# A gated MLP fed with x times the norm's weights, its factor applied to the products, and weight splits kept two tiles ahead beside modulation rows

## Chip, cores and metric

The kernel runs on one core of one Trainium2 chip. The metric is the device time of one execution in microseconds (us): the median of several runs. TensorE is called PE (its weight loads PEld), VectorE DVE, ScalarE ACT, GpSimd POOL, SyncE SP.

## What is computed

A first block of two layers, and then a second block of two layers, on 256 tokens of width 1024 in fp32 (the first block carries 256 context tokens too). Cut to what matters here:

```python
def first_block(...):
    for l in range(DEPTH):                                 # DEPTH = 2
        mod_x = silu(c) @ w_ada[l] + b_ada[l]              # 6 * 1024 modulation values, for x
        mod_c = silu(c_ctx) @ w_ada[l] + b_ada[l]          # and for the context
        ...attention, x = x + gt1 * (o @ w_out[l])
        hx2 = rms_norm(x, g_norm2[l]) * (1 + sc2) + sh2
        x = x + gt2 * conv_ffn(hx2, ...)

def second_block(...):
    for l in range(DEPTH):
        ...four branches, merged
        x = x + rms_norm_2(merged @ w_out[l], norm_mix_post[l])
        h2 = rms_norm_2(x, norm_ffn_pre[l])                # x * rsqrt(mean(x*x) + eps) * g
        f_g, f_u = split(h2 @ w_ffn_in[l], 2)              # 2 * 2816 columns
        f = (silu(f_g) * f_u) @ w_ffn_out[l]
        x = x + rms_norm_2(f, norm_ffn_post[l])
```

The factor `rsqrt(mean(x*x))` is one number for each token, so `h2 @ w` equals `((x * g) @ w)` times that number.

## The kernel before

Activations lie transposed: 8 chunks of 128 channels by 256 tokens. A product in fp32 accuracy is three matmuls in fp32r: weights and activations are each the sum of a rounded high part and a low part, and hi*hi, hi*lo and lo*hi are added (`products`, L396 to L398). One weight tile is 128 x 1024 (8 blocks of 128 x 128) and gives 128 output channels with 24 matmuls.

**The stream of weights.** All weights come as one list of 704 tiles of up to 512 KB. SP loads tile i into one of NRAW = 6 raw buffers as soon as the tile six before it is used up (for a tile that is to be split: when its low part is made; for a modulation tile, which is never split: when its matmuls are done). The tiles to be split then go through ACT (high part, L968) and DVE (low part, L1572) into one of NSPLIT = 4 buffers, which come free when the matmuls of the tile four before are done. Every engine runs through the same program order with its own `Feed`. `Feed.next()` is called where a tile is used, and there it issues, in order, the splits that are due: up to five list places ahead of the tile in use, as long as the buffer's last user has been released.

```python
    def next(self):
        i = self.n
        self.n += 1
        while self.cut < min(i + NRAW, self.total) and self.room():
            if self.cut in self.place:
                self.split(self.cut)
            self.cut += 1
        return i
```

The queues of ACT and DVE are thus in this order by hand: a split stands where `next` was called, with its wait on the load (ACT) or on the high part (DVE), and what comes after it waits behind it.

**Modulation rows.** `ada_step` takes two weight tiles, does 8 fp32 matmuls with 2 active rows (L482), and DVE copies the 128 x 256 result out of PSUM (L1634). One call later `ada_turn` has PE transpose it in two halves (L467), and DVE adds four pieces of 32 rows (L1619) and the bias (L1622). 8 steps are at the start; the others are put between the units of the first block's attention, one for each unit, until they are used up: 12 beside layer 0's first stream, 12 beside its second, 10 beside layer 1's (4 and 2 more stand just ahead). During attention they are the only tiles of the stream; the output projection's 8 tiles follow in the list. In one attention unit PE does the scores (L572), the turn of the row before (L467), values (L606, L611), transposes of probabilities (L591) and then the matmuls of the next modulation row (L482). DVE's queue in the same unit: maxima, the copies out of PSUM (L1771 among them), then the splits of `next`, then the copy of the row (L1634).

**Output projection** of the first block: for each of 8 tiles DVE adds to the residual x (L1582, XT<-ps), ACT squares it (L1006), and PE sums the squares (L453). ACT's queue begins with the load of the Sqrt table (`warm`, L996), and then has for each tile: `next` (splits), square. DVE's has: `next` (splits), residual. After the eighth tile come the root (ACT L1024), its reciprocal (DVE L1608), and the norm.

**The gated MLP of the second block**, layer l: `post_add` on DVE updates x in four pairs of chunks (L2224, L2229). ACT squares each chunk (L1006), PE sums the 8 squares with a matrix of ones in fp32 (L453), ACT takes the root (L1024), DVE the reciprocal (L1608), DVE multiplies x by weight and factor (`norm2`, L1582), ACT makes the high parts (L1326), DVE and POOL the low ones (L1999, L2284). PE's first two tiles (`two_tiles`) do the parts that need high parts alone (L410, L411), 32 matmuls, and then those with low parts (L416), 16. From then on 22 steps j have a gate tile, an up tile and a tile of the down projection five steps behind. Between them: ACT Silu of the gate product (L1553), DVE times the up product (L2243), POOL the high and the low part (L2539, L2541).

## Time and profile before

| | |
|---|---|
| median of 3 runs | 2309.62 us (2307.52 to 2311.8) |
| profiled execution, its own time | 2310.19 us |
| its span, first to last instruction | 2308.1 us |
| mean granted clock of TensorE | 0.965 |
| PE busy | 2141.5 us (93%) |
| DVE busy | 1552.1 us (67%) |
| ACT busy | 1151.8 us (50%) |
| POOL busy | 489.6 us (21%) |
| DMA | 378.21 MB, mean 164 GB/s |

Engines overlap, so the shares don't add up. Where PE is busy without a break, only fewer or shorter matmuls help; elsewhere the time is set by the chain that ends each of its waits. The clock is that of the matmul array, as a share of 2.4 GHz; at 0.50 a matmul takes twice the time between starts.

### The profile page before, as it was taken

The page shows a single profiled execution, that of the slowest core. Times are in us where ns is not written, and L with a number is a line of the kernel's source. Part 1 is how long each engine was busy: PE and PEld are TensorE (multiplying, and loading weights), DVE is VectorE, ACT ScalarE, POOL GpSimd, SP SyncE. Part 2 cuts the span into 40 slices and gives each one's busy share as a digit, 9 for nine tenths or more (in the row PEclk, how much of TensorE's full clock was granted, in tenths as well). Part 3 has the DMA queues.
Part 4 walks back from the last instruction along what each step waited for, and adds up shares of the span by engine and source line. Part 5 has one row for each costly group of instructions (what it writes and reads, how often), then busy time and mean ns, then how long its engine had stood idle before and what let it go on. Part 6 is the DMA issues. An engine that isn't in the chain of part 4 may idle for free.

```text
span 2308.1 us, 42283 instructions
## 1 busy us (share of the span) xinstructions
PE 2141.5 (93%) x17432; PEld 1970.9 (85%) x17432; DVE 1552.1 (67%) x2301; ACT 1151.8 (50%) x1917; POOL 489.6 (21%) x628
## 2 busy tenths in 40 slices
PE   6999979999999998899998989989998999998998
PEld 3985549999999995589997889989997888998997
DVE  3657766777777756667776769756555677965554
ACT  3534444555655642555556555554444655554443
POOL 0011330333233002213321043202110124311110
PEclk8999999999999998999999999999999999998999
DMA  8535444555465443335553435544553433553552
GB/s 325 164 128 220 165 183 146 178 195 177 155 201 185 153 165 128 147 119 188 187 190 104 157 104 191 173 138 164 185 190 103 146 128 129 165 185 127 191 191 84
DMA packets 103199, 378.21 MB, mean 164 GB/s; under 512 B 11584, under 2 KB 11744, under 8 KB 101984
## 3 DMA queue, kind: packets, MB, share of 16 engines
q1 hardware_dynamic: 101520, 367.31, 46.7%
q10 hardware_dynamic: 1488, 8.20, 0.9%
q8 instruction: 139, 2.28, 0.4%
q14 instruction: 52, 0.43, 0.1%
HBM read 374.42 MB, written 1.05 MB: 163 GB/s over the span
## 4 chain that ended last, share of the span: by engine, by line
PE 35%; issue 8%; DVE 6%; POOL 3%; ACT 3%; POOLq 0%; DVEq 0%; ACTq 0%
PE ps L396 10%; PE ps L397 10%; PE ps L398 10%; DVE WL L1572 2%; PE ps L453 2%; POOL R L2521 1%; POOL R L2479 1%; ACT WH L968 1%; DVE RST L1608 1%; DVE TMP L1582 1%; PE ps L410 1%; DVE R L1582 1%; PE ps L411 1%; PE ps L416 0%; POOL X L2284 0%
## 5 line engine op out<-in xcount | busy, mean ns | idle before, releaser
L396 PE MATMUL ps<-X,WH 128*128 128x256 f32 x4384 | 1243.4, 284 | 13.6 <-DVE WL L1572 12.5
L397 PE MATMUL ps<-X,WH 128*128 128x256 f32 x4384 | 1228.7, 280 | 0.0
L398 PE MATMUL ps<-X,WL 128*128 128x256 f32 x4384 | 1225.8, 280 | 0.0
L1572 DVE TENSOR_TENSOR WL<-RAW,WH 128x1024 fp32r<-128x1024 f32 (+2 forms) x608 | 802.7, 1340 | 461.3 <-ACT WH L968 460.6
L396 PEld LDWEIGHTS ps<-X,WH 128*128 128x128 f32 x4384 | 826.9, 189 | 28.3 <-DVE WL L1572 17.6
L397 PEld LDWEIGHTS ps<-X,WH 128*128 128x128 f32 x4384 | 827.4, 189 | 1.4
L398 PEld LDWEIGHTS ps<-X,WL 128*128 128x128 f32 x4384 | 827.1, 189 | 0.0
L968 ACT ACTIVATE WH<-RAW 128x1024 fp32r<-128x1024 f32 (+2 forms) x608 | 625.7, 1047 | 383.7 <-PE ps L398 362.5
L1106 ACT ACTIVATE PB<-ps,SM 128x512 f32<-128x512 f32 (+1 forms) x152 | 87.7, 584 | 156.4 <-DVE SM L1745 156.2
L2326 POOL TENSOR_SCALAR R<-CONS,SM 128x128 f32<-128x128 f32 x128 | 84.4, 670 | 360.5 <-DVE SM L1755 360.5
L2418 POOL TENSOR_TENSOR TMP<-TMP 128x256 f32<-128x256 f32 x66 | 49.0, 742 | 438.3 <-ACT TMP L1288 434.8
L1582 DVE SCALAR_TENSOR_TENSOR TMP<-ps,PARS,TMP 128x255 f32<-128x255 f32 x264 | 124.2, 480 | 9.5 <-ACT TMP L1284 0.6
L1582 DVE SCALAR_TENSOR_TENSOR R<-R,PARS 128x256 f32<-128x256 f32 x180 | 109.5, 660 | 0.0
L2423 POOL TENSOR_TENSOR X<-TMP,X 128x256 fp32r<-128x256 f32 x66 | 104.0, 1576 | 5.3
L1284 ACT ACTIVATE TMP<-ps,PARS 128x256 f32<-128x256 f32 x132 | 71.4, 555 | 55.9 <-PE ps L398 52.8
L410 PE MATMUL ps<-X,WH 128*128 128x256 f32 x208 | 64.4, 337 | 25.5 <-ACT X L1326 14.0
L1745 DVE TENSOR_REDUCE SM<-ps 128x1 f32<-128x512 f32 (+2 forms) x136 | 77.1, 605 | 14.5 <-PE ps L572 13.9
L1288 ACT ACTIVATE TMP<-TMP 128x256 f32<-128x256 f32 x66 | 27.8, 421 | 113.1 <-DVE TMP L1582 113.1
L606 PE MATMUL ps<-PTB,R 128*64 128x128 f32 x768 | 61.5, 293 | 24.4 <-ACT PTB L1121 16.8
L606 PEld LDWEIGHTS ps<-PTB,R 128*64 128x64 f32 x768 | 44.8, 143 | 45.5 <-issue 20.5
L482 PE MATMUL ps<-RAW,R 128*32 128x256 f32 x768 | 62.3, 444 | 22.3 <-DVE R L1619 8.5
L2539 POOL CAST X<-TMP 128x256 fp32r<-128x256 f32 x44 | 19.4, 442 | 282.1 <-DVE TMP L2243 282.1
(184 smaller groups left out, 2157.5 us busy)
## 6 DMA issues: line engine op xcount, KB each, us to landing
RAW<-w_dram SPq DMA_DIRECT2D x674, 512.0 KB, 3.8
RAW<-w_dram SPq DMA_DIRECT2D x16, 480.0 KB, 3.1
BIG<-big_dram ACTq DMA_DIRECT2D x4, 1024.0 KB, 5.1
RAW<-w_dram SPq DMA_DIRECT2D x8, 320.0 KB, 2.7
RAW<-w_dram SPq DMA_DIRECT2D x6, 384.0 KB, 3.0
XT<-x_dram ACTq DMA_DIRECT2D x2, 1024.0 KB, 10.9
CONS<-con_dram ACTq DMA_DIRECT2D x1, 1105.0 KB, 5.0
out_dram<-XT SPq DMA_DIRECT2D x1, 1024.0 KB, 3.9
```

Source lines behind the costliest of these rows:

```text
L396: e.matmul(out, a.hi, b.hi, start=start and i == 0, stop=False, skip_group_check=open_bank)
L397: e.matmul(out, a.hi, b.lo, start=False, stop=False, skip_group_check=open_bank)
L398: last = e.matmul(out, a.lo, b.hi, start=False, stop=stop and i == n - 1, skip_group_check=open_bank)
L410: e.matmul(b.ap[:, 0:256], w.hi[:, c], src[c].hi, start=c == 0, stop=False)
L606: e.matmul(ob[0].ap[64 * s:64 * s + 64, c:c + 128], u["subs"][s]["v"][j], b[:, 128 * j:128 * j + 128], start=j == 0, stop=j == nk - 1)
L968: e.activation(weights(i).hi, raw(i), ACT.Copy).then_inc(*w_hi.mark(i))
L1106: e.activation(ap, bank.ap[:, x * u["nk"]:x * u["nk"] + u["nk"]], ACT.Exp, bias=sm.ap[:, col:col + 1], accum_out=sm.ap[:, 4 + col:5 + col] ...
L1572: e.tensor_tensor(weights(i).lo, raw(i), weights(i).hi.bitcast(F32), ALU.subtract).then_inc(*w_lo.mark(i))
L1582: return e.scalar_tensor_tensor(out=out, in0=a, scalar=s, in1=b, op0=o0, op1=o1)
L1745: e.tensor_reduce(sm.ap[:, col:col + w], bank.ap[:, 0:w * nk].rearrange("p (x n) -> p x n", x=w), AX, ALU.max, negate=True).then_inc(*maxe ...
L2326: e.tensor_scalar(d.ap, ident, sm.ap[:, 8 + s:9 + s], None, ALU.mult).then_inc(*inverted.mark(tag, i, s))
L2423: e.tensor_tensor(a.ap.lo, bg.ap, a.ap.hi.bitcast(F32), ALU.subtract).then_inc(*gate_lo.mark(tag, j))
```

## The change

1. In the second block the MLP's input is x times the norm's weights: ACT makes the high parts straight from x with the weight as scale, in pairs, as `post_add` finishes them, then the squares of the same pair; DVE makes the low parts. PE starts the first two tiles' high parts at once, then sums the squares (`between`), then does the low parts. The factor goes on the gate product twice: DVE multiplies it out of PSUM (`scaled`), ACT takes the Silu in place, POOL multiplies the result by the factor again (`pooled`), which stands for the factor of the up product; DVE times the up product as before. So per step j there is one DVE and one POOL instruction more, and Silu waits for DVE; the 8 multiplications of `norm2` and its 8 copies become 8 scaled copies.
2. Beside modulation rows after the first eight, `Feed.next` splits up to two places ahead (`ahead=3`) and not five.
3. The turn of a modulation row is two fp32 matmuls with a 128 x 2 picking matrix as moving operand, which sum the four pieces as well; DVE's reduction is gone, the bias is added straight from PSUM.

```diff
@@ class Feed
-    def next(self):
+    def next(self, ahead=NRAW):
         i = self.n
         self.n += 1
-        while self.cut < min(i + NRAW, self.total) and self.room():
+        while self.cut < min(i + ahead, self.total) and self.room():
...
@@ tensor: two_tiles(src, at, between=None)
                         e.matmul(b.ap[:, 0:256], w.lo[:, c], src[c].hi, start=False, stop=False)
+                if between is not None:
+                    between()
                 for b, i in zip(bk, us):
...
@@ tensor: ada_turn, ada_step
                 for h in range(2):
-                    last = e.transpose(bank.ap[:, 256 + 128 * h:384 + 128 * h], b.ap[:, 128 * h:128 * h + 128], ident)
+                    last = e.matmul(bank.ap[:, 256 + 2 * h:258 + 2 * h], b.ap[:, 128 * h:128 * h + 128], con("pick"), start=True, stop=True)
                 last.then_inc(*adaturn.mark(l, c))
-                bank.free = [modded("sum", l, c)]
+                bank.free = [modded(l, c)]
-            def ada_step(ring=PS):
+            def ada_step(ring=PS, ahead=3):
...
-                    i = feed.next()
+                    i = feed.next(ahead)
...
             for c in range(8):
-                ada_step()
+                ada_step(PS, NRAW)
...
@@ tensor: second block
-                ss = SquareSum(("fpre", l), 8)
-                for n in range(4):
+                ss = SquareSum(("fpre", l), 8, k.sq2[0])
+                for _ in range(8):
                     ss.add()
-                    ss.add()
-                    ss.flush(keep=2)
-                ss.rstd(k.rst[0])
-                feed_forward(("glu", l), parts2_of(("fpre", l)), lambda tag, j, half: (convd if half else gated)(tag, j, half))
+                feed_forward(("glu", l), parts_of(("fpre", l)), lambda tag, j, half: convd(tag, j, half) if half else scaled(tag, j),
+                             between=lambda: ss.rstd(k.rst[1]))
...
@@ scalar: second block
-                ss = SquareSum(("fpre", l), 8)
-                post_add(("post", l), ss)
-                ss.rstd(1024, k.rst[0])
-                norm2(("fpre", l))
-
-                def silu_gate(j, bk):
-                    (bank, i), _ = bk
+                k.rst[0].free = [scaled(("post", l), "s", 3)]
+                ss = SquareSum(("fpre", l), 8, k.sq2[0])
+                for n in range(4):
+                    q.wait_ge(*resid(("post", l), n))
+                    for c in (2 * n, 2 * n + 1):
+                        e.activation(H.hi[:, c], X2[:, c], ACT.Copy, scale=par("fpre", l)[:, c:c + 1]).then_inc(*x_hi.mark(("fpre", l), c))
+                    for c in (2 * n, 2 * n + 1):
+                        ss.add(X2[:, c])
+                ss.rstd(1024, k.rst[1])
+
+                def silu(j):
                     b = tmp.take()
-                    q.wait_ge(*lin(i))
-                    wait(b.free)
-                    e.activation(b.ap, bank.ap[:, 0:256], ACT.Silu).then_inc(*gated.mark(("glu", l), j, 0))
+                    q.wait_ge(*scaled(("glu", l), j))
+                    e.activation(b.ap, b.ap, ACT.Silu).then_inc(*gated.mark(("glu", l), j, 0))
                     b.free = [gate_lo(("glu", l), j)]
...
@@ vector: ada_turn
-                t = ADA[c % 2]
-                parts = bank.ap[:, 256:512].rearrange("p (h j m) -> p h m j", h=2, j=4)[:, :, 0:2, :]
-                e.tensor_reduce(t, parts, AX, ALU.add).then_inc(*modded.mark("sum", l, c))
-                q.wait_ge(*modded("sum", l, c))
+                parts = bank.ap[:, 256:260].rearrange("p (h s) -> p s h", h=2)
                 b_ada = par("b_ada", l)[:, 2 * c:2 * c + 2].unsqueeze(1).to_broadcast([128, 2, 2])
-                e.tensor_tensor(MODS[l][:, :, 2 * c:2 * c + 2], t.rearrange("p h s -> p s h"), b_ada, ALU.add).then_inc(*modded.mark(l, c))
+                e.tensor_tensor(MODS[l][:, :, 2 * c:2 * c + 2], parts, b_ada, ALU.add).then_inc(*modded.mark(l, c))
...
@@ vector: second block
-                ss.rstd(k.rst[0])
-                norm2(("fpre", l), par("fpre", l), recips(("fpre", l)))
+                for c in range(8):
+                    q.wait_ge(*x_hi(("fpre", l), c))
+                    stt(H.lo[:, c], X2[:, c], par("fpre", l)[:, c:c + 1], H.hi[:, c].bitcast(F32), ALU.mult,
+                        ALU.subtract).then_inc(*x_lo.mark(("fpre", l), c))
+                ss.rstd(k.rst[1])
+                bufs = {}
+
+                def silu_in(j, bk):
+                    b = bufs[j] = tmp.take()
+                    (bank, i), = bk
+                    q.wait_ge(*recips(("fpre", l)))
+                    q.wait_ge(*lin(i))
+                    wait(b.free)
+                    e.tensor_tensor(b.ap, bank.ap[:, 0:256], k.rst[1].ap, ALU.mult).then_inc(*scaled.mark(("glu", l), j))
 
                 def silu_gate(j, bk):
-                    b, (bank, i) = tmp.take(), bk[1]
-                    q.wait_ge(*gated(("glu", l), j, 0))
+                    b, (bank, i) = bufs.pop(j), bk[1]
+                    q.wait_ge(*pooled(("glu", l), j))
                     q.wait_ge(*lin(i))
...
-                feed_forward(("glu", l), silu_gate)
+                feed_forward(("glu", l), silu_gate, first=silu_in)
...
@@ gpsimd: second block
-                norm2(("fpre", l))
+                bufs = {}
+
+                def scale_gate(j):
+                    b = bufs[j] = tmp.take()
+                    q.wait_ge(*recips(("fpre", l)))
+                    q.wait_ge(*gated(("glu", l), j, 0))
+                    e.tensor_tensor(b.ap, b.ap, k.rst[1].ap, ALU.mult).then_inc(*pooled.mark(("glu", l), j))
...
@@ constants
+    put("pick", np.tile(np.eye(32)[:, 0:2], (4, 1)))
```

`feed_forward` on ACT, DVE and POOL gets an argument `first`, called when the gate tile's product is taken and before the `next` of the up tile.

## Rows read from the trace of the kernel before

**Rows 1.** Waits: engine, line, waited for: us in total, times, longest.

```profile
ACT WH L968 <- DMA RAW<-w_dram: 19.8, 8, 5.4
...
PEld ps L467 <- DVE R L1634: 55.4, 39, 6.7
```

**Rows 2.** Timeline of PE, layer 0, second stream: start, us, line, [idle before <- releaser].

```profile
290.29 1.07 PE L482 MATMUL ps<-RAW,R 128*32 128x256 f32 x16
...
293.69 1.07 PE L482 MATMUL ps<-RAW,R 128*32 128x256 f32 x16
...
295.32 0.44 PE L467 MATMUL ps<-CONS,R 128*128 128x128 f32 x2
...
305.56 1.07 PE L482 MATMUL ps<-RAW,R 128*32 128x256 f32 x16
...
312.30 0.69 PE L467 MATMUL ps<-CONS,R 128*128 128x128 f32 x2 [5.04 <-DVE R L1634]
...
329.83 0.70 PE L572 MATMUL ps<-R 64*128 64x256 f32 x4
```

**Rows 3.** Timeline of ACT in the same stretch.

```profile
309.60 1.06 ACT L968 ACTIVATE WH<-RAW 128x1024 fp32r<-128x1024 f32 x1 [5.10 <-DMA RAW<-w_dram]
```

**Rows 4.** Timeline of DVE in the same stretch.

```profile
293.80 0.69 DVE L1771 COPY PTB<-ps 128x512 f32<-128x512 f32 x1 [0.58 <-PE ps L591]
...
310.69 1.23 DVE L1572 TENSOR_TENSOR WL<-RAW,WH 128x1024 fp32r<-128x1024 f32 x1 [3.89 <-ACT WH L968]
```

**Rows 5.** Timeline of PE, layer 1's attention.

```profile
927.25 1.07 PE L482 MATMUL ps<-RAW,R 128*32 128x256 f32 x16
...
931.95 1.07 PE L482 MATMUL ps<-RAW,R 128*32 128x256 f32 x16
...
937.19 1.07 PE L482 MATMUL ps<-RAW,R 128*32 128x256 f32 x16
...
957.41 0.70 PE L711 MATMUL ps<-RST,CONS 32*128 32x256 f32 x4
...
965.00 1.13 PE L572 MATMUL ps<-R 64*128 64x512 f32 x4
```

**Rows 6.** Timeline of DVE, layer 1's output projection.

```profile
991.92 0.49 DVE L1582 SCALAR_TENSOR_TENSOR XT<-ps,SM,XT 128x256 f32<-128x256 f32 x1 [2.05 <-PE ps L398]
...
994.98 0.48 DVE L1582 SCALAR_TENSOR_TENSOR XT<-ps,SM,XT 128x256 f32<-128x256 f32 x1
...
1013.70 0.48 DVE L1582 SCALAR_TENSOR_TENSOR XT<-ps,SM,XT 128x256 f32<-128x256 f32 x1
```

**Rows 7.** Timeline of ACT, layer 1's output projection: end of the table's warming.

```profile
991.63 0.21 ACT L996 ACTIVATE SM<-CONS 128x1 f32<-128x1 f32 x1
```

**Rows 8.** Timeline of PE's weight loads, layer 0's second output projection.

```profile
389.30 0.19 PEld L396 LDWEIGHTS ps<-X,WH 128*128 128x128 f32 x1 [1.21 <-DVE WL L1572]
```

**Rows 9.** Timeline of all engines, start of the second block's first MLP.

```profile
1549.53 6.25 PE L453 MATMUL ps<-PB,CONS 128*128 128x256 f32 x16 [4.73 <-ACT PB L1006]
...
1558.63 2.01 ACT L1326 ACTIVATE X<-TMP 128x256 fp32r<-128x256 f32 x5 [2.34 <-DVE TMP L1582]
...
1559.19 0.55 PE L410 MATMUL ps<-X,WH 128*128 128x256 f32 x1 [3.42 <-ACT X L1326]
...
1565.76 2.04 PE L416 MATMUL ps<-X,WH 128*128 128x256 f32 x16
...
1567.65 0.28 PE L396 MATMUL ps<-X,WH 128*128 128x256 f32 x1
```

**Rows 10.** Busy time by windows: length, PE, PEld, DVE, ACT, POOL, PEclk, DMA share, GB/s.

```profile
1564.00:1566.00 2.00, 2.00 (x16) 2.00 (x14) 1.55 (x3) 0.56 (x1) 0.00 (x0) 0.77 0.00 0
...
1570.00:1740.00 170.00, 170.00 (x1446) 170.00 (x1445) 93.35 (x82) 69.39 (x81) 25.60 (x43) 1.00 0.56 189
```

**Rows 11.** One line of the kernel each: duration ns min/median/max, first and last start.

```profile
L2418 POOL TENSOR_TENSOR TMP<-TMP x66: 727/743/753, 403.9 to 1193.9; 128x256 f32<-128x256 f32 x66
```

**Rows 12.** The same view for the reduction of a modulation row.

```profile
L1619 DVE TENSOR_REDUCE R<-ps x48: 142/159/175, 14.4 to 963.5; 128x4 f32<-128x16 f32 x48
```

More of the change, by code:

```diff
@@ L987, in tile, with used @@
                 return PS.take(), i
-            def used():
-                i = feed.next()
+            def used(ahead=NRAW):
+                i = feed.next(ahead)
                 feed.release(i)
@@ L1135, in attend, with feed_forward @@
                 highs(units[n - 1]["tile"])
-            def feed_forward(tag, gate, early=None, late=None):
+            def feed_forward(tag, gate, early=None, late=None, first=None):
                 bk, steps = [], iter(())
@@ L1142, in feed_forward @@
                         bk.append(got.pop(0) if got else tile())
+                        if len(bk) == 1 and first is not None:
+                            first(j)
                         if len(bk) == 2:
@@ L1799, in attend, with feed_forward @@
                         invert(i)
-            def feed_forward(tag, gate, early=None, late=None):
+            def feed_forward(tag, gate, early=None, late=None, first=None):
                 bk, steps = [], iter(())
@@ L1806, in feed_forward @@
                         bk.append(got.pop(0) if got else tile())
+                        if len(bk) == 1 and first is not None:
+                            first(j, bk)
                         if len(bk) == 2:
@@ L2344, in feed_forward @@
                         bk += 1
+                        if bk == 1 and first is not None:
+                            first(j)
                         if bk == 2:
```

42 lines of the change are left out of this document (21 added, 21 removed).

## The prediction

> **What bounds the kernel now.** The first view is the page's busy time. PE is busy for 93% of the span, so the time is PE's work plus its waits. The next question is where PE is busy without a break, because there only its own work counts. The windows over a gated MLP answer it. PE has 170.00 us of work in 170 us, with DVE at 93.35, ACT at 69.39 and POOL at 25.60 [rows 10]. Instructions added on those three engines are free there as long as no wait reaches PE.
>
> Then the waits, for the gaps. Two belong to this change. ACT waited up to 5.4 us for a raw weight tile, and PE's loads for the transposed modulation row waited 55.4 us for DVE's copy of it [rows 1]. The timelines tie them together. Beside the last three modulation rows of layer 0's second stream, ACT's next entry is the split of an output projection tile that is not loaded yet. It idles 5.10 us and starts at 309.60 [rows 3]. DVE's low part follows at 310.69 after 3.89 us of idling [rows 4]. The copy of the modulation row stands behind that split, so PE stops for 5.04 us before L467 at 312.30 [rows 2]. The wait of an early split is thus paid by PE through two queues. The same happens beside layer 1's last rows.
>
> The third place is the start of the second block's MLP. PE idles 4.73 us before the sums of squares. It does them in 6.25 us, idles 3.42 us, and starts the first tile at 1559.19; its third tile starts at 1567.65 [rows 9]. It is also slow there: the granted clock is a mean of 0.77 in 1564 to 1566, against 1.00 in the loop behind [rows 10]. The 32 matmuls from 1559.19 to 1565.76 take 0.205 us each, and the 16 after them 0.118 [rows 9]. That is the 1.2 GHz level and the 2.4 GHz level.
>
> **Part 1: splits two ahead beside modulation rows.** Splits of the projection's tiles 1 to 4 were spread over the last three rows. Now only tiles 1 and 2 are split, both beside the last row, when their loads have had two units to land. Tiles 3 and 4 move to the start of the projection.
>
> *Layer 0, second stream.* An undisturbed unit takes 3.40 us (L482 at 290.29, again at 293.69). From L482 at 305.56 to the first scores after the last row, 329.83, are three units: 24.27 us in place of 10.20 [rows 2]. Surplus 14.07. What stays is a wait in the last unit. Let that unit begin at L482 = 0. ACT makes two high parts of 1.06, so the second is done at 2.1. DVE's copy L1771 ends at 0.8 (294.49 against 293.69), so its second low part runs from 2.1 to 3.35 (1.23 long). The copy of the row adds 0.38, which is the distance from the low part's end at 311.92 to L467 at 312.30: 3.75. L467 normally starts at 1.63. PE waits about 2.1 [rows 2 to 4]. Gain 14.07 - 2.1 = 12.0.
>
> *Layer 1.* A unit takes 4.70 us (927.25 to 931.95). From 937.19 to 965.00 are three units and one extra group of 0.63 (0.70 less the overlap): 27.81 in place of 14.73, surplus 13.08 [rows 5]. ACT has a copy of probabilities before the splits here, so I take 2.5 for the wait that stays. Gain 10.6. Both gains could be up to 2 smaller if splits and exponentials collide, and up to 2 larger if the remaining wait vanishes.
>
> *What it costs later.* In the projection, DVE's first residual now stands behind the low parts of tiles 3 and 4, and ACT's high parts for them start only after the table is warm, at 991.84 [rows 7]. Two high parts end at 993.95, the second low part at 995.2. So the first residual is at about 995.3 instead of 991.92, 3.4 late. Behind it, residual, square, high part and low part form a ring of one tile: 3.06 us (991.92 to 994.98). Before, the eighth residual came 21.78 us after the first (1013.70) [rows 6]; the ring alone needs 7 x 3.06 = 21.4. So 0.4 is caught up, and the eighth residual is 3.0 late. Root, reciprocal and norm hang on it with PE idle, so layer 1 pays 3.0. I add 0.5, because a longer pause leaves the array at 1.2 GHz for longer: 3.5. In layer 0 a second projection follows as cover. But PE already waits there for low parts (1.21 before one tile [rows 8]), so the delay passes through: 2.9. PE's tile 3 needs its low part 5.6 us after the projection starts, which is about when it is ready; a wait there costs 0 to 1.5 for each layer. If no delay were passed on, both costs would be 0.
>
> **Part 2: the start of the MLP, twice.** The first pair of chunks is ready as before, so PE begins at about 1549.5, but with tile 1 instead of sums. ACT makes 8 copies and 8 squares of 0.40 (five in 2.01 [rows 9]), somewhat less for squares: the last pair's copies end near 1554.5. PE's first tile trickles along with them and ends near 1555. Tile 2 is 16 matmuls of 0.205: 1558.3. The sums take 6.25 at 1.2 GHz and about half at 2.4. After the last pause the full clock came back some 5.7 us after work began, so it should come back during tile 2 or the sums here: I take 4.0 and get 1562.3. The low parts take 1.9: third tile at 1564.2 instead of 1567.65, a gain of 3.4. I count 3.0, since the first tile's gaps may delay the clock. Bounds: 1.2 with all sums at the low level, 5.7 with the full clock from 1555 on. Two layers: 6.0 (2.4 to 11.4).
>
> Root, reciprocal and the first multiplication now lie beside PE's low parts and third and fourth tiles; the fourth tile's split stands behind ACT's root and DVE's reciprocal, but is due two tiles later. In the loop DVE gets 22 more multiplications and POOL 22 more of 0.743 [rows 11] for each layer. DVE has 76 us free of 170 and POOL 144 [rows 10]: price nothing. If the cover were gone, 44 x 0.743 = 33 us would be due.
>
> The Trainium skill, page "SBUF — State Buffer" (the shared port pair), says that a GpSimd instruction and a DVE instruction with two SBUF inputs exclude each other, so the added POOL work could hold up DVE's splits. By that rule DVE loses at most the same 33 us over both loops, against 2 x 76 us free, so it would change nothing here.
>
> **Part 3: the modulation turn.** A pair of transposes takes 0.44 us [rows 2]. The new turn is two fp32 matmuls, each two instructions in this trace (the 8 modulation matmuls are x16). Lower bound: 1.07/16 = 0.067 each, 0.27 for four. Upper bound: as long as a transpose each, 0.88; two moving columns can't take longer than 128. Over 28 rows where PE is the bound that is -5 to +12. Each of the four still loads 128 columns, so I take no change. DVE loses a reduction of 0.16 [rows 12] in 34 rows. Most of it falls into idle time; I take 0.9 in all. PE's next row waits for the bank until the bias is added instead of the sum, which is the same place in DVE's queue.
>
> The Trainium skill, page "TensorE: Matmul & The Clock Gate", section "LDWEIGHTS (loading the stationary operand)", gives a load as columns / 1.2 ns: 107 ns for 128, whatever follows it. By it four loads make 0.43 us as an estimate, which speaks against any gain from the short moving operand. No row shows this shape; the sum above does not use it.
>
> **Sum.** -12.0 - 10.6 + 2.9 + 3.5 - 6.0 - 0.9 = -23.1 us. On the profiled execution's 2310.2 that is 2287.1; it lies 0.6 above the median, so 2286.5 for the median.
>
> **Rivals.**
> *The waits come back in the projections* (0.15). PE reaches tile 3 before its late split in both layers, and layer 0's second projection stays behind DVE: 4 to 5 us more in each layer. Speaking for it: the ring of 3.06 has almost no slack and PE already waits for low parts [rows 6, 8]. Against: PE's squares slow it to more than the ring. Time 2286.5 + 9 = 2295.5.
> *More is gained* (0.13): the array stays at 2.4 GHz around the sums, and the delay of the projection is absorbed. -23.1 - 5 - 4: 2277.5.
> *The distance does nothing* (0.05): ACT waits for the same loads later, so only parts 2 and 3 count, and the later splits' delay does not appear. -6.9: 2302.7.
> *Slower* (0.05): in the MLP loop Silu waits for DVE, POOL for Silu, DVE for POOL, and DVE's next split stands behind that. If the round trip exceeds its cover, every j is longer. It decides at 23.1/44 = 0.53 us for each j; if the 0.743 of POOL's new multiplication showed in full, the time is 2286.5 + 33 = 2319.5. Against it: DVE and ACT have 3.5 and 4.6 us free in each j [rows 10], and splits are three tiles ahead.
> *The forecast* (0.62): 2281 to 2292.
>
> The forecast, more gained and most of the first rival give the range 2277 to 2298. 0.2%, or 4.6 us, is about what a measurement of this kernel can tell from no change. Slower is the fourth rival, 0.05. Within it: 0.02, the part of the third rival in which part 2 gives its lower bound too. Faster: the rest, 0.93.
>
> **What the new profile would show.** ACT's splits with waits for RAW beside the last modulation rows gone, PE's waits before the turn at most 2.5 us. First residual of the projections about 3.4 us later behind the attention's end. At the MLP's start L410 before L453 and no 3.42 us gap. The MLP loops still with PE at 100%. Wrong would be: waits of PE for low parts in the projections above 2 us, a loop longer than before, or a turn that takes longer than 0.44.

## The result, and the profile after

The changed kernel takes 2294.34 us (median of 4 runs, 2292.43 to 2298.63) against 2308.57 for the kernel before on the same chip: ratio 0.994, 95% interval 0.9921 to 0.9959. That is 14.2 us less, where 23.1 were forecast (2286.5 us, range 2277 to 2298). The profiled execution of after took 2298.63, its span is 2296.8, so it is the slowest of its runs. One execution of experiment 10 (4141 us) and one of the kernel before beside it (4162 us) were disturbed, and no ratio counts them. In what follows, a difference between kernels is the ratio of the runs less one, times 2310 us, with its interval; a difference between places of two traces is said to be one.

The waits of the page after (engine, line, waited for: total, times, longest), beside [rows 1]:

```profile
PEld ps L468 <- DVE R L1636: 37.2, 39, 4.6
...
PE ps L395 <- DVE WL L1577: 21.9, 19, 2.8
...
PE ps L468 <- DVE R L1636: 13.2, 9, 4.1
```

L1636 is the copy of the row, L468 the new turn, L1577 the low part, L395 the first product. Beside the modulation rows ACT's waits for a raw tile are gone; 5.1 us of such waits are left, all in the first 40 us. The wait before the turn shrank and did not vanish. PE's wait for low parts over the whole kernel stood like this before:

```profile
PE ps L396 <- DVE WL L1572: 18.3, 16, 3.3
```

It grew by 3.6 us. Its long cases lie outside the first block's output projections, where none is longer than 1.2 us. PE's timeline in layer 0's second stream, beside [rows 2]:

```profile
311.45 1.07 PE L483 MATMUL ps<-RAW,R 128*32 128x256 f32 x16
312.45 0.70 PE L573 MATMUL ps<-R 64*128 64x256 f32 x4
313.09 0.61 PE L468 MATMUL ps<-CONS,R 128*128 128x2 f32 x4
313.62 0.66 PE L607 MATMUL ps<-PTB,R 128*64 128x128 f32 x8
...
315.01 1.07 PE L483 MATMUL ps<-RAW,R 128*32 128x256 f32 x16
...
318.58 1.07 PE L483 MATMUL ps<-RAW,R 128*32 128x256 f32 x16
...
323.53 1.01 PE L468 MATMUL ps<-CONS,R 128*128 128x2 f32 x4 [3.25 <-DVE R L1636]
324.47 1.12 PE L607 MATMUL ps<-PTB,R 128*64 128x128 f32 x8
...
326.99 1.23 PE L573 MATMUL ps<-R 64*128 64x256 f32 x4
```

Read the starts, not the durations, for the price of a stretch. From the turn's start to the next instruction are 0.53 us here (313.09 to 313.62; the median of the turns at the full clock is 0.54), and 0.37 before (L467 at 295.32, the next line at 295.69). The unit is 3.56 long (311.45 to 315.01), not 3.40. Behind the 3.25 us wait everything takes nearly twice as long: L607 1.12 for 0.66, L468 itself 1.01 for 0.61. The granted clock is 0.50 from the turn to the next scores. DVE and ACT in the last unit, beside [rows 3, 4]:

```profile
318.22 2.00 ACT L967 ACTIVATE WH<-RAW 128x1024 fp32r<-128x1024 f32 x2
```

```profile
318.98 1.29 DVE L1911 TENSOR_TENSOR X<-R,X 128x256 fp32r<-128x256 f32 x2
320.19 0.68 DVE L1773 COPY PTB<-ps 128x512 f32<-128x512 f32 x1
320.79 2.35 DVE L1577 TENSOR_TENSOR WL<-RAW,WH 128x1024 fp32r<-128x1024 f32 x2
323.06 0.41 DVE L1636 COPY R<-ps 128x256 f32<-128x256 f32 x1
```

ACT's two splits start without a wait for the load. But DVE had two low parts of the attention's output to make (L1911, 1.29 us) before its copy L1773, which ends at 320.9, 2.3 after the unit's start, where the prediction had put it at 0.8. The two low parts then follow in one piece, and the row's copy behind them.

Layer 1's projection on DVE, beside [rows 6]. From the scores behind the last row to the first residual are 30.95 us (962.11 to 993.06), against 26.92 before (965.00 to 991.92), so 4.0 more. Of these, 0.9 are the scores themselves, which run at the half clock here (962.11 to 964.02). In experiment 1 below, where they don't, it is 3.2 more. The ring is the same, 3.06:

```profile
990.78 2.36 DVE L1577 TENSOR_TENSOR WL<-RAW,WH 128x1024 fp32r<-128x1024 f32 x2 [2.96 <-ACT WH L967]
993.06 0.48 DVE L1587 SCALAR_TENSOR_TENSOR XT<-ps,SM,XT 128x256 f32<-128x256 f32 x1
...
996.12 0.48 DVE L1587 SCALAR_TENSOR_TENSOR XT<-ps,SM,XT 128x256 f32<-128x256 f32 x1
...
1014.46 0.48 DVE L1587 SCALAR_TENSOR_TENSOR XT<-ps,SM,XT 128x256 f32<-128x256 f32 x1
```

The start of the second block's first MLP, and the windows of its loop, beside [rows 9, 10] (length, then busy time of PE, PEld, DVE, ACT, POOL, then PEclk, DMA share, GB/s):

```profile
1551.85 0.55 PE L409 MATMUL ps<-X,WH 128*128 128x256 f32 x1 [4.91 <-ACT X L1549]
...
1555.99 0.58 PE L409 MATMUL ps<-X,WH 128*128 128x256 f32 x1 [0.19 <-ACT X L1549]
...
1560.42 4.00 PE L454 MATMUL ps<-R,CONS 128*128 128x256 f32 x16
1564.07 2.22 PE L417 MATMUL ps<-X,WH 128*128 128x256 f32 x16
1566.13 0.28 PE L395 MATMUL ps<-X,WH 128*128 128x256 f32 x1
```

```profile
1570.00:1740.00 170.00, 170.00 (x1460) 170.00 (x1459) 92.58 (x105) 71.47 (x84) 64.57 (x65) 1.00 0.56 193
```

The first tile starts where the sums stood, in steps of ACT's pairs, the sums take 3.7 us at a mean granted clock of 0.89, and the third tile starts 14.28 us after PE's wait (1551.85 to 1566.13), against 18.12 before (1549.53 to 1567.65). The loop is still all PE, with POOL at 65 in place of 26.

### The profile page after: what moved, and what is told of

Same layout as the page of the kernel before. It is cut to its first block, busy times and chain, and to the rows that moved or that the text cites. A ratio compares the mean times of both kernels' runs of the same rounds, so it can differ in the third digit from the quotient of the medians.

```text
span 2296.8 us, 42538 instructions
## 1 busy us (share of the span) xinstructions
PE 2151.5 (94%) x17528; PEld 1987.3 (87%) x17528; DVE 1532.2 (67%) x2285; ACT 1152.5 (50%) x1917; POOL 565.1 (25%) x668
## 4 chain that ended last, share of the span: by engine, by line
PE 36%; issue 8%; DVE 5%; POOL 3%; ACT 3%; POOLq 0%; DVEq 0%; ACTq 0%
PE ps L395 11%; PE ps L397 10%; PE ps L396 10%; DVE WL L1577 2%; POOL R L2539 1%; PE ps L454 1%; POOL R L2497 1%; ACT WH L967 1%; DVE RST L1613 1%; PE ps L409 1%; DVE R L1587 1%; PE ps L410 1%; PE ps L417 1%; DVE TMP L1587 1%; POOL X L2300 0%
## 5 line engine op out<-in xcount | busy, mean ns | idle before, releaser
L395 PE MATMUL ps<-X,WH 128*128 128x256 f32 x4384 | 1241.8, 283 | 16.9 <-DVE WL L1577 16.0
L1577 DVE TENSOR_TENSOR WL<-RAW,WH 128x1024 fp32r<-128x1024 f32 (+2 forms) x608 | 782.5, 1307 | 455.3 <-ACT WH L967 454.6
L395 PEld LDWEIGHTS ps<-X,WH 128*128 128x128 f32 x4384 | 826.2, 188 | 31.5 <-DVE WL L1577 21.2
L409 PE MATMUL ps<-X,WH 128*128 128x256 f32 x208 | 66.5, 344 | 29.2 <-ACT X L1549 10.6
L607 PE MATMUL ps<-PTB,R 128*64 128x128 f32 x768 | 60.8, 291 | 25.2 <-ACT PTB L1120 17.7
L2557 POOL TENSOR_TENSOR TMP<-TMP,RST 128x256 f32<-128x256 f32 x44 | 32.8, 745 | 209.6 <-ACT TMP L1557 209.6
L607 PEld LDWEIGHTS ps<-PTB,R 128*64 128x64 f32 x768 | 44.4, 142 | 41.5 <-issue 15.7
```

What stands on the lines that cost most here:

```text
L395: e.matmul(out, a.hi, b.hi, start=start and i == 0, stop=False, skip_group_check=open_bank)
L409: e.matmul(b.ap[:, 0:256], w.hi[:, c], src[c].hi, start=c == 0, stop=False)
L607: e.matmul(ob[0].ap[64 * s:64 * s + 64, c:c + 128], u["subs"][s]["v"][j], b[:, 128 * j:128 * j + 128], start=j == 0, stop=j == nk - 1)
L1577: e.tensor_tensor(weights(i).lo, raw(i), weights(i).hi.bitcast(F32), ALU.subtract).then_inc(*w_lo.mark(i))
```

## The experiments

ACT computes the same 32 square roots in every kernel, so their starts are milestones by which traces can be laid over each other. The table gives the start in the trace of before, and for each kernel the shift against it in us. Column heads are the experiments' numbers below. Experiment 10 isn't among them: its trace is that of the execution of 4141 us.

| root at | after | 1 | 2 | 3 | 4 | 5 | 6 | 7 | 8 | 9 | 11 | 12 |
|---|---|---|---|---|---|---|---|---|---|---|---|---|
| 157.4 | +0.7 | -0.9 | -1.3 | +2.6 | -0.5 | -0.7 | +6.8 | +0.5 | -0.1 | -0.7 | -1.4 | -0.5 |
| 226.0 | +3.8 | -1.0 | -2.2 | +9.2 | -0.6 | -0.8 | +18.1 | -0.2 | -0.2 | -0.1 | -2.3 | -0.5 |
| 298.3 | +5.8 | -2.4 | -2.3 | +8.9 | -2.0 | +0.6 | +21.5 | -0.6 | -0.2 | -1.5 | -3.7 | -0.7 |
| 370.2 | +0.6 | -8.1 | -2.6 | +11.5 | -7.8 | -4.0 | +17.2 | -6.9 | -9.8 | -8.0 | -9.5 | -7.6 |
| 829.3 | +1.9 | -8.4 | -2.8 | +11.5 | -8.2 | -2.8 | +17.1 | -6.9 | -10.1 | -8.1 | -9.9 | -7.7 |
| 1015.4 | +1.3 | -16.5 | +0.2 | +18.0 | -16.2 | -6.0 | +18.8 | -15.3 | -22.0 | -13.8 | -17.8 | -15.7 |
| 1466.1 | +2.5 | -12.9 | +0.5 | +15.7 | -18.2 | -8.8 | +17.0 | -14.4 | -21.4 | -14.4 | -20.0 | -17.7 |
| 1753.8 | -3.2 | -12.3 | -5.1 | +15.9 | -22.6 | -14.3 | +12.9 | -19.8 | -26.8 | -20.4 | -25.8 | -23.8 |
| 2012.8 | -7.4 | -11.9 | -9.7 | +17.8 | -21.8 | -16.3 | +13.7 | -24.1 | -31.0 | -19.8 | -27.5 | -28.7 |
| 2296.6 | -11.3 | -10.1 | -13.3 | +18.4 | -25.9 | -19.5 | +9.7 | -28.0 | -35.0 | -23.0 | -31.3 | -34.4 |

The first modulation rows lie before 157, layer 0's rows from 157 to about 320, layer 1's from 829 to 950. The MLPs of part 2 lie in 1466 to 1754 and in 2013 to 2297.

Each column is one execution. The stretch from 1753.8 to 2012.8, which no part edits, shows how far that goes: it moves by -5.0 (experiment 12) to +1.9 (experiment 3) against before. The time at half clock in it, worked out as twice the length times what the mean granted clock lacks to 1, is 13.7 us in the first of them and 34.1 in the second.

**Experiments 1 to 4: the parts alone.** First each of the three parts on the kernel before, then parts 1 and 2 together, that is the changed kernel without the new turn. Their diffs are cut from that of the change.

*1, part 1 alone:*

```diff
+    def next(self, ahead=NRAW):
+        while self.cut < min(i + ahead, self.total) and self.room():
...
+            def ada_step(ring=PS, ahead=3):
```

> Only part 1: splits two places ahead beside modulation rows; turn and MLP as before. Theory A (from the two traces: the three units with splits shrink from 24.27 to about 15.2 us in layer 0 and from 27.81 to about 19.4 in layer 1, half clock behind the last row costs 0.8 each, later residuals cost 2.7 and 3.3): 10 us faster than before. Rival B (the forecast's sizes, with a wait of 2.1 to 2.5 us beside the last row): 16 us faster. Rival C (the splits only move their waits): within 2 us of before.

Ratio 0.9937 (0.992 to 0.9953): -14.6 us. That is rival B's size; theory A's 10 lies just outside the interval, and rival C is refuted.

*2, part 2 alone:*

```diff
-                norm2(("fpre", l))
+                        e.activation(H.hi[:, c], X2[:, c], ACT.Copy, scale=par("fpre", l)[:, c:c + 1]).then_inc(*x_hi.mark(("fpre", l), c))
```

> Only part 2: the second block's MLP on x times the weights, factor on the products. Theory A (third tile of each MLP 3.5 and 4.0 us earlier in the traces, loops unchanged): 7.5 us faster. Rival B: the loops with DVE and POOL instructions added give back part of it, 3 us faster or less. Rival C: 11 us faster, if the 1.9 us gained in the first loop and the 3.7 us between the layers in the profiled execution belong to the change.

Ratio 0.9946 (0.993 to 0.9963): -12.5 us, more than theory A's 7.5. Rival C's 11 is within the interval, rival B is refuted.

*3, part 3 alone:*

```diff
-                    last = e.transpose(bank.ap[:, 256 + 128 * h:384 + 128 * h], b.ap[:, 128 * h:128 * h + 128], ident)
+                    last = e.matmul(bank.ap[:, 256 + 2 * h:258 + 2 * h], b.ap[:, 128 * h:128 * h + 128], con("pick"), start=True, stop=True)
```

> Only part 3: the picking matmul in place of the transposes. Theory A: the turn takes 0.53 us of PE in place of 0.37 in each of some 40 rows where PE is the bound, 6 to 7 us slower, and no change in the clock. Rival B: the short matmuls also keep the array longer at half clock at the start of attention (17 us in place of 8 in the profiled execution), 9 to 10 us slower. Rival C (the forecast): no change, 0.9 us faster.

Ratio 1.0058 (1.0041 to 1.0075): +13.4 us. That is above theory A's 6 to 7, rival B's 9 to 10 stand at the edge of the interval, and rival C, the forecast, is refuted.

*4, parts 1 and 2*, the edits of 1 and 2 together:

> Parts 1 and 2 with the transposes kept. Theory A: 17 to 18 us faster than before, 2291, that is some 6.5 faster than the changed kernel adds up to without the turn's price. Rival B: the parts don't add up, because half clock phases move with every shift; then within 3 us of the changed kernel's 14 us.

Ratio 0.986 (0.9841 to 0.9879): -32.3 us. Neither theory had it: A said 17 to 18, B about 14.

The three parts add up to -13.7, and the whole change is -13.9 by its ratio. Parts 1 and 2 add up to -27.1, and together they measure -32.3. Each ratio is uncertain by some 4 us, so no acting on each other is shown. The new turn costs 13.4 us on the kernel before and 18.4 on parts 1 and 2, where the prediction had a gain of 0.9. Part 1 came out as forecast (-16.2), part 2 gave more than its 6.0.

**Experiments 5 to 7: what the new turn costs.** By PE's starts, a turn takes 0.17 us more than before. That is 8 us over 48 rows, and not 13 or 18. The granted clock was a candidate for the rest: in 180 to 200 it was 0.57 after, and 0.83 before.

*5, a wide moving operand*, on the changed kernel:

```diff
-  last = e.matmul(bank.ap[:, 256 + 2 * h:258 + 2 * h], b.ap[...], con("pick"), ...)
+  last = e.matmul(bank.ap[:, 256 + 128 * h:384 + 128 * h], b.ap[...],
+                  con("pick").unsqueeze(1).to_broadcast([128, 64, 2]), ...)
```

> The changed kernel, with the picking matrix of the turn given as a moving operand of 128 columns in place of 2 (the same two columns repeated 64 times); the result is the same. Theory A: a turn costs what its four instructions and their loads of 128 columns cost, 0.134 us each, whatever the moving operand is; so L468 x4 stays at 0.61 and the time stays within 3 us of the changed kernel (ratio to it 1.000). Theory B: the short moving operand makes the array look idle and keeps it at 1.2 GHz longer (17 us in 180 to 200 in place of 8); with 128 columns the stretch is short again and the kernel is 5 to 8 us faster than the changed one. Theory C: the moving columns count as well; a turn gets longer by 0.05 or more for each instruction, and the time rises by 10 us or more.

*6, each matmul of the turn twice*, on the changed kernel:

```diff
                 for h in range(2):
+                    e.matmul(bank.ap[:, 256 + 2 * h:258 + 2 * h], b.ap[...], con("pick"), start=True, stop=True)
                     last = e.matmul(...)
```

> The changed kernel with each matmul of the turn issued twice (same bank, same result): eight instructions in place of four beside each of 48 rows. Theory A (0.134 us for each instruction, nothing else): 48 x 4 x 0.134 = 25.7 us slower than the changed kernel, up to 4 more where the clock is halved. Theory B (the cost lies mostly in the clock: 7.9 of about 15 us are time of instructions, the rest slow stretches that the small matmuls lengthen): 35 us or more slower, with half clock in stretches where the changed kernel had the full one.

*7, one matmul of the turn in place of two*, on the changed kernel:

```diff
-  for h in range(2):
+  for h in range(1):
...
-  parts = bank.ap[:, 256:260].rearrange("p (h s) -> p s h", h=2)
+  parts = bank.ap[:, 256:258].unsqueeze(2).to_broadcast([128, 2, 2])
```

> The changed kernel with one of the two matmuls of each turn; the modulation values of the second 128 channels of a row are copies of the first, so that half of a row's sums is left out. Two instructions, 0.27 us, against 0.53 in the changed kernel and 0.37 for the transposes. Theory A: 48 x 0.267 = 12.8 us faster than the changed kernel, so about 2281.5, within 4 us of the kernel without the new turn (2279.9), and rather 4 us faster than that. Theory B (small matmuls halve the clock whatever their number): 3 to 7 us faster than the changed kernel alone, and still 8 or more behind the kernel without the new turn.

Ratios 0.9909 (0.9893 to 0.9925), 1.004 (1.0026 to 1.0054) and 0.9884 (0.9866 to 0.9902). Against the changed kernel that is -7 us for the wide operand, +23 for the doubled turn and -13 for the half one. PE's starts around a turn at the full clock, wide, twice and half:

```profile
288.64 0.71 PE L468 MATMUL ps<-CONS,R 128*128 128x128 f32 x4
289.28 0.66 PE L608 MATMUL ps<-PTB,R 128*64 128x128 f32 x8
```

```profile
296.13 0.38 PE L468 MATMUL ps<-CONS,R 128*128 128x2 f32 x2
...
297.12 0.66 PE L608 MATMUL ps<-PTB,R 128*64 128x128 f32 x8
```

```profile
288.04 0.38 PE L468 MATMUL ps<-CONS,R 128*128 128x2 f32 x2
288.35 0.66 PE L607 MATMUL ps<-PTB,R 128*64 128x128 f32 x8
```

By the medians over all turns at the full clock, two instructions take 0.31 us, four 0.54, eight 0.98, and four with 128 moving columns 0.64. So the 2 columns save a sixth against 128, and each instruction costs 0.11 besides an entry of 0.09. Then the clock, windows 170 to 230 (length, PE busy, PEclk, DMA share, GB/s), for the kernels before, after, wide, twice and half, in this order, and last for experiments 4 and 11, which are one kernel:

```profile
170.00:230.00 60.00, 54.09 (x510) 0.94 0.57 210
```

```profile
170.00:230.00 60.00, 56.41 (x496) 0.86 0.54 193
```

```profile
170.00:230.00 60.00, 54.15 (x531) 1.00 0.58 211
```

```profile
170.00:230.00 60.00, 56.17 (x415) 0.77 0.46 160
```

```profile
170.00:230.00 60.00, 54.06 (x514) 0.94 0.60 211
```

```profile
170.00:230.00 60.00, 54.48 (x512) 0.94 0.59 212
```

```profile
170.00:230.00 60.00, 52.59 (x522) 1.00 0.58 212
```

The last two windows warn that one kernel can show 0.94 or 1.00 here. The eight traces with transposes have 0.91 to 1.00. The wide turn's 1.00 and the half turn's 0.94 are within that. Below it are the three kernels with four or eight two-column instructions a turn: 0.86, 0.77, and 0.80 in experiment 3. In the table, the wide turn is 4.6 us ahead of the changed one at the root at 226.0 (-0.8 against +3.8), and 7.3 at 1015.4, where 4 and 11 are 1.6 apart. The medians alone would not show it, since 4 and 11 differ by as much (6.7 us, below).

The root at 1015.4 has all 48 turns behind it. The table gives the lag behind experiment 4 there, what 48 turns cost by their starts against transposes, what is left of the lag, and the time at half clock from the root at 157.4 on, all in us:

| turn | instructions | start to start | lag | by starts | rest | at half clock |
|---|---|---|---|---|---|---|
| after | 4 | 0.54 | 17.5 | 8.1 | 9.4 | 66.5 |
| wide | 4, of 128 columns | 0.64 | 10.2 | 13.2 | -3.0 | 44.4 |
| twice | 8 | 0.98 | 35.0 | 29.5 | 5.5 | 66.5 |
| half | 2 | 0.31 | 0.9 | -2.6 | 3.5 | 44.4 |

In the traces of the six kernels with transposes and part 1 (experiments 1, 4, 8, 9, 11, 12) that time is 30.7 to 47.8 us. The wide turn costs no more than its instructions' time. The two-column turn costs 9.4 us more than that and stands at half clock 18.7 us longer than the highest of the six. Twice as many instructions don't double this: the same 66.5 us, and a smaller rest.

One place shows the halving by itself, the last row of layer 1. PE's timeline there, of the changed kernel, of experiment 4 and of the wide turn:

```profile
956.97 0.98 PE L468 MATMUL ps<-CONS,R 128*128 128x2 f32 x4 [2.30 <-DVE R L1636]
...
962.11 1.98 PE L573 MATMUL ps<-R 64*128 64x512 f32 x4
```

```profile
943.40 0.44 PE L469 MATMUL ps<-CONS,R 128*128 128x128 f32 x2 [2.30 <-DVE R L1640]
...
946.03 1.13 PE L574 MATMUL ps<-R 64*128 64x512 f32 x4
```

```profile
951.75 0.71 PE L468 MATMUL ps<-CONS,R 128*128 128x128 f32 x4 [2.30 <-DVE R L1637]
...
956.28 1.13 PE L574 MATMUL ps<-R 64*128 64x512 f32 x4
```

The wait is 2.30 in all three. With the transposes the array stays at the full clock behind it (so in experiments 1, 4, 11 and 12), and so it does with the half turn. With four two-column instructions it falls to half, and the same work takes 5.14 us in place of 2.63. But with four 128-column instructions it falls too, a little later, and the work takes 4.53; with eight it takes 4.03. So at this place the width of the moving operand doesn't decide. What decides stays open.

So both theories hold part of it: experiments 6 and 7 follow the time of the instructions (A), and the first rows of experiment 5 the clock (B). Theory A's "within 3 us" for the wide operand is refuted by the traces (7.3 us at the root at 1015.4), and so is B for the doubled turn (35 or more).

**Experiments 8 to 10 and 12: what is left in parts 1 and 2.** All are built on experiment 4.

*8, the splits in the last units of attention.* Nothing is split beside later rows (`ahead=1`). In the last stream of a layer, the calls of `ada_next` behind the last row each split one tile, on ACT from the 14th call on, on DVE from the 15th:

```diff
+    def fill(self):
+        while self.cut < min(self.n + 4, self.total) and self.room():
+            self.cut += 1
+            if self.cut - 1 in self.place:
+                self.split(self.cut - 1)
+                break
...
+                        elif st == streams[-1] and unit[0] >= 13:    # 14 on DVE
+                            feed.fill()
+                        unit[0] += 1
```

> Parts 1 and 2 without the new turn (2279.9 us), and then: no split at all beside modulation rows; the four splits of the projection stand one by one in the last units of attention, behind the rows (ACT from its 14th call on, DVE from its 15th). Theory A: the wait that was left before the last turn (3.24 and about 2.3 us) goes, with about 0.8 us of half clock behind each, and the first residual of each projection comes 2.5 to 3 us earlier: 8 to 12 us faster than parts 1 and 2, about 2270. Theory B: DVE has no room in these units (2.0 us of its own work of 2.6, and 1.23 for a low part), so its copies of the probabilities come later and PE waits there for them: 0 to 4 us faster. Theory C: it is slower.

Ratio 0.9859 (0.9842 to 0.9875), -32.6 us. PE's and DVE's timeline in layer 0:

```profile
314.86 0.44 PE L476 MATMUL ps<-CONS,R 128*128 128x128 f32 x2 [0.97 <-DVE R L1652]
...
325.68 1.07 PE L615 MATMUL ps<-PTB,R 128*64 128x128 f32 x8 [1.87 <-DVE PTB L1789]
```

```profile
322.20 1.22 DVE L1590 TENSOR_TENSOR WL<-RAW,WH 128x1024 fp32r<-128x1024 f32 x1
...
324.85 0.68 DVE L1789 COPY PTB<-ps 128x512 f32<-128x512 f32 x1
...
334.55 0.48 DVE L1600 SCALAR_TENSOR_TENSOR XT<-ps,SM,XT 128x256 f32<-128x256 f32 x1 [1.86 <-PE ps L405]
```

The wait before the last turn is 0.97 for 3.24 in experiment 4, and the first residual stands at 334.55 for 337.11. At the same time PE waits 1.87 us for a copy of probabilities that the low part at 322.20 pushed back. By the table, layer 0's attention and projection (root 298.3 to 370.2) take 3.8 us less than in experiment 4, and layer 1's (829.3 to 1015.4) 3.9 less. So theory A's two terms are there, and theory B's collision eats part of them: 7.7 us in these two stretches, where A had 8 to 12. At the root at 298.3, ahead of them, experiment 8 is 1.8 behind experiment 4, so at 1015.4 it is 5.8 ahead in all. In the medians the gain over experiment 4 drowns in what the two batches differ by (below).

The last four kernels ran together.

*9, no split beside rows, none in the last units:*

```diff
-            def ada_step(ring=PS, ahead=3):
+            def ada_step(ring=PS, ahead=1):
```

> Parts 1 and 2 without the new turn, with no split beside the later modulation rows (ahead=1), so that the four splits due all stand at the start of the output projection. Theory A (what the earlier run of the splits at the end shows as two terms, a wait before the last turn and a later residual, trade against each other): the wait of 3.24 us before the last turn falls to about 1.0 and takes 0.7 us of half clock with it, but PE's first tile waits for its low part and the first residual stands behind four low parts in place of two, 2.2 to 3.4 us later; both layers together within 3 us of parts 1 and 2. Theory B (a late residual is absorbed by the projections): 5 to 7 us faster than parts 1 and 2. Theory C (both PE's late start and the late residual are paid): 4 to 8 us slower.

*10, DVE's low parts one unit later than in 8:*

```diff
-                        elif st == streams[-1] and unit[0] >= 14:
+                        elif st == streams[-1] and unit[0] >= 15:
```

> The kernel with the splits in the last units of attention, but DVE's low parts one unit later (from its 16th call on, so three in the last units and the fourth at the projection's start). There the low part of DVE's 15th call ended just ahead of the maxima and pushed the next copy of probabilities back; PE waited 1.87 us for it, and the clock was halved after that. Theory A: that wait shrinks by 0.8 to 1.2 us in each layer and the slow stretch starts later or not at all, while the first residual comes 0.5 us later: 0 to 4 us faster than with the splits one unit earlier, so 4 to 8 us faster than parts 1 and 2 in this batch. Theory B: the remaining waits are those of the drain itself: same within 1 us as the run with the splits one unit earlier, in the roots of the first block.

*11, parts 1 and 2 again:*

> Parts 1 and 2 without the new turn once more, so that the other three stand beside it on one chip. Earlier ratio 0.986 [0.9841, 0.9879]; expected again within 0.2% of it. It also tells how far the stretches that no edit touches (the loops at 0.1160 or 0.1171 us for each matmul) move between two sets of runs of one kernel: theory A, they are fixed by the kernel's text and come out the same; theory B, they differ from execution to execution by 1 to 4 us over a few hundred us.

*12, PE's sums ahead of the first two tiles:*

```diff
                 bk = [PS.take() for _ in us]
+                if between is not None:
+                    between()
                 for b, i in zip(bk, us):
```

> Parts 1 and 2 with PE's sums of squares ahead of the first two tiles of the second block's MLP (as they were before), everything else of part 2 kept: scaled copies straight from x, the factor on the products. Theory A (the gain comes from the norm's multiplications leaving the chain; the order on PE only fills a wait): the sums trickle with the squares until about 6.5 us after the first pair, then 32 matmuls, 5 to 6.6 us, and 1.9 for the low parts: third tile 14 to 15 us after the start of the wait's end, within 1.5 us for each MLP of the kernel with the tiles first. Theory B (the gain is the sums hidden behind the trickling tile): 3 us or more slower for each MLP, 6 or more in all.

| | ratio | interval | us |
|---|---|---|---|
| 9 | 0.9889 | 0.9875 to 0.9904 | -25.6 |
| 10 | 0.9826 | 0.9805 to 0.9846 | -40.2 |
| 11 | 0.9889 | 0.9873 to 0.9905 | -25.6 |
| 12 | 0.9863 | 0.984 to 0.9887 | -31.6 |

Experiment 9 has the ratio of 11, as theory A had it. In layer 0 it gains 0.7 us (root 298.3 to 370.2: -6.5 against -5.8), in layer 1 it loses 2.2 (829.3 to 1015.4: -5.7 against -7.9). An early split that blocks a queue and a late one that delays the residuals cost about the same here.

Experiment 10 is the fastest kernel of the study, 14.6 us below 11 with intervals that don't meet, and by the ratios 26 below the changed kernel. The only trace of it is that of the 4141 us, so none shows why it gains more than the 4 to 8 us expected. That stays open. Part of it may be the scatter of executions: the five of experiment 12 lie between 2275.60 and 2287.49.

Experiment 12 is no slower: its first MLP (root 1466.1 to 1753.8) gains 6.1 us against before, that of 4 and 11 gains 4.4 and 5.8; its second gains 5.7 against 4.1 and 3.8. So theory A holds: the order of sums and tiles on PE is not what brings part 2's gain. What is left of the edit is that the norm's multiplications left the chain; no run takes that alone. In both MLPs experiment 12 stands 6.8 us at half clock, 4 and 11 stand 10.2, which is worth up to 1.7 us each and covers most of its lead.

Experiments 4 and 11 are the same kernel. Their ratios are 6.7 us apart, 0.29% where at most 0.2% was expected, their traces 5.4 at the last root, and in the first block at most 1.7. Part of the difference is the speed of loops in which PE never waits. Windows in the two MLP loops, experiment 4 and then 11:

```profile
1650.00:1700.00 50.00, 50.00 (x426) 50.00 (x426) 29.22 (x31) 20.80 (x24) 11.33 (x18) 1.00 0.57 189
2150.00:2200.00 50.00, 50.00 (x431) 50.00 (x430) 26.24 (x30) 20.70 (x24) 17.77 (x18) 1.00 0.56 190
```

```profile
1650.00:1700.00 50.00, 50.00 (x431) 50.00 (x430) 26.51 (x30) 20.97 (x24) 17.37 (x19) 1.00 0.56 186
```

In the same loop one execution did 426 matmuls in 50 us and the other 431, both with PE always busy and the clock at 1.00. Theory B holds: for this kernel it is the execution, not the text.

## Why the prediction was right and wrong

The direction and the range held. The gain was 9 us smaller than forecast, by two large errors of opposite sign and a small one. That the total stayed in the range is in part luck. The measured 2294.3 lies outside the 2281 to 2292 that had the chance of 0.62, and next to the first rival's 2295.5, but that rival's mechanism did not occur. Of the signs named for being wrong one came true: the turn lasts 0.61 us, above 0.44.

**The step that failed is part 3's price**, "I take no change" for the pair of transposes. The value between the bounds was taken as 0.44; four instructions measured 0.54 from start to start, where the two transposes take 0.37. The figure of 0.44 was the transposes' duration and not the distance of two starts, and so it hid that four instructions with four loads were not free. Its range "-5 to +12 over 28 rows" did hold the instructions' share: 48 x 0.17 = 8.1.

What it lacked altogether is the clock. By the traces the new turn costs 17.5 us up to layer 1's projection (after less experiment 4 at the root at 1015.4). Of these, 1.2 fall to the start, 40 x 0.17 = 6.8 to the instructions of the later rows (28 in layer 0, 12 in layer 1), and 1.7 to the stretch from 370.2 to 829.3, in which no row is turned. The 7.8 that are left lie beside the rows, where 63 us are at half clock in place of 34; 2.3 of them are in the one place shown above. That the clock costs them is worked out by difference, not isolated: the wide turn, which has no such rest, halves the clock in that place as well. By the ratios the turn costs 13.4 (experiment 3), 18.4 (4) or 11.7 (11, the same kernel as 4).

In the prediction the Trainium skill (page "TensorE: Matmul & The Clock Gate", section on LDWEIGHTS) spoke for 107 ns a load, 0.43 for four. The sequence 0.31, 0.54, 0.98 for two, four and eight instructions has that slope, 0.11, and an entry of 0.09 on top; the runs agree with the rule for the short operand. What misled was the comparison with the transposes' 0.44.

**Part 1 was nearly right in sum, with two errors that went the same way in layer 0.** Forecast were -9.1 and -7.1 for the two layers, the waits less the later residuals. Experiment 1 shows -5.7 (298.3 to 370.2; -7.2 from 157.4 on) and -8.1 (829.3 to 1015.4). In layer 0 "PE waits about 2.1" was 3.25, because DVE's copy L1771 was timed from an undisturbed unit, and the last unit has two more low parts before it. Then the wait also halved the clock for the rest of the unit: 3.5 us from the turn's start to the next scores (323.53 to 326.99) where a full clock needs 1.9, which no term had. The wait in layer 1 was 2.30 for 2.5 forecast. The later residuals cost what they were said to. In layer 1 the first is 3.2 late in experiment 1, for 3.4 forecast, and 4.0 in after, where 0.9 belong to the slow scores. Of that the ring of 3.06 caught up 0.4, as forecast: in after the eighth residual is 52.35 us behind the scores (1014.46), before 48.70 (1013.70). The first rival, waits of 4 to 5 us more in each projection, did not occur: PE's waits for L1577 before L395 add up to 2.9 us in 330 to 400, for 1.2 before, and none stands in layer 1's projection. Layer 0 is 3.4 short of its forecast, layer 1 is 1.0 better. "The distance does nothing" is refuted by experiment 1.

**Part 2 was undersized.** The third tile came 14.3 us after PE's start, forecast 14.7 (1549.5 to 1564.2), before 18.1: 3.8 us, of which the prediction worked out 3.4 and then counted 3.0 out of caution. By the roots, experiment 2 gained 5.6 and 3.7 us in the two MLPs, less up to 2 us for the loops' own drift. So 7 to 9 of the 12.5 us of its ratio are seen in the MLPs, where 6.0 were forecast. In the same trace 4.6 us more lie between the MLPs, where nothing was edited and the time at half clock is 13.7 us for 27.3 before. So at least part of the 6.5 that the ratio is above the forecast need not be part 2's doing. Experiment 12 speaks for the cause named, the norm off the chain, by excluding the order on PE. The loop's price of nothing held, with POOL at 65 us of 170; the fourth rival (slower by the round trip) did not occur, nor did the exclusion of GpSimd and DVE that the Trainium skill's page "SBUF — State Buffer" states reach PE (170.00 us busy of 170).

By the ratios the terms are -14.6, -12.5 and +13.4, forecast were -16.2, -6.0 and -0.9. The errors are +1.6, -6.5 and +14.3, and together the 9 us that were missing.

## What to carry to other kernels

Price an instruction by the distance of starts in its own neighbourhood, and count instructions and loads of the replacement before counting its columns: a reduction folded into a matmul is no gain if it doubles the loads. Where the granted clock changes within a stretch, ask what a new instruction does to the clock as well as to the queue, and look at two traces of one kernel before reading a change into one window. When a blocking entry of an in-order queue is moved later, time its new place from the unit in which it will stand, and look for a slot where the queue idles (the drain of a pipeline) and not only a shorter distance.

## What was not expected of the hardware

- Beside turns of four or eight two-column instructions the array stood longer at half clock: 66.5 us between the roots at 157.4 and 1015.4, for 30.7 to 47.8 in the six traces with transposes and part 1, and 44.4 with four 128-column instructions. The turn that did more work (128 columns) brought that stretch to its end 7.3 us earlier. It is no simple rule: eight a turn gave the same 66.5 as four, and behind the 2.30 us wait in layer 1 the clock was halved with 128 columns too. The Trainium skill (page "TensorE: Matmul & The Clock Gate", the part on the clock gate) says that the gate goes by how busy the array has been. The profile's busy share doesn't tell these windows apart: 54.15 us of 60 beside a clock of 1.00, 54.09 beside 0.94.
- At a granted clock of 1.00 the same loop runs at one of two speeds, 426 or 431 matmuls in 50 us (0.1174 or 0.1160 us each), for hundreds of us, and which one is a matter of the execution. It moves an MLP by up to 2 us and, with the half clock between the MLPs, blurs comparisons of 0.1 to 0.3%. What sets it stays open.
